# Two model stacks in one kernel: other orders in the recurrent block and in the second stack's attention, and splits moved or made narrower

## The reference

```python
gate, u = jnp.split(x @ w_in, 2, axis=-1)
u = causal_depthwise_conv(u, conv_w, conv_b)                 # 4 taps
r = sigmoid(blocks(u) @ w_rgate + b_rgate)                   # 4 blocks of 256 features
i = sigmoid(blocks(u) @ w_igate + b_igate)
log_a = -LRU_C * r * softplus(-lam)
b_in = sqrt(-expm1(2 * log_a)) * (i * u)
h_t = exp(log_a)_t * h_(t-1) + b_in_t                        # a scan over the tokens
y = (h * gelu(gate)) @ w_o
```

## Time and profile before

| | us |
|---|---|
| median of 3 runs | 2154.22 (2153.88 to 2158.78) |
| the profiled execution | 2156.41 |
| its span | 2155.1 |
| PE busy | 2062.3 (96%) |
| DVE busy | 1540.4 (71%) |
| ACT busy | 1177.7 (55%) |
| POOL busy | 68.5 (3%) |

### The profile page before, as it was taken

How to read it: one execution, slowest core, us unless ns; L and a number is a source line. 1 busy time by engine, 2 the same in 40 slices (tenths; PEclk the granted TensorE clock), 3 DMA queues, 4 the chain that set the end, 5 groups by cost and what they waited for, 6 DMA issues and landing times.

```text
span 2155.1 us, 33112 instructions
## 1 busy us (share of the span) xinstructions
PE 2062.3 (96%) x13325; PEld 1860.2 (86%) x13325; DVE 1540.4 (71%) x2678; ACT 1177.7 (55%) x2047; POOL 68.5 (3%) x121
## 2 busy tenths in 40 slices
PE   7999999898999989999998999999989999989998
PEld 7878899796899978889987789998978999878997
DVE  4685776888677776677777867778466777666776
ACT  4555555484465556456554545655455655565654
POOL 3000000010000010000000000001000000000000
PEclk9999999999999999999999999999999999999999
DMA  8424566455366654457654346665525765524763
GB/s 270 145 90 147 171 203 189 143 165 181 120 199 196 190 147 132 139 154 216 191 179 140 104 143 213 205 186 161 158 69 158 214 204 178 168 85 135 220 178 118
DMA packets 411849, 355.81 MB, mean 165 GB/s; under 512 B 16163, under 2 KB 353319, under 8 KB 411697
## 3 DMA queue, kind: packets, MB, share of 16 engines
q1 hardware_dynamic: 405104, 332.49, 50.5%
q0 software_dynamic: 6592, 21.21, 3.0%
HBM read 352.61 MB, written 1.05 MB: 164 GB/s over the span
## 4 chain that ended last, share of the span: by engine, by line
PE 80%; DVE 13%; ACT 4%; issue 1%; DMA 1%; POOL 0%; SPq 0%; DVEq 0%; ACTq 0%
PE psum L715 19%; PE psum L717 18%; PE psum L716 18%; PE psum L1228 15%; DVE w_lo L1825 3%; PE psum L1121 3%; PE psum L1107 1%; DVE qt L2260 1%; PE psum L1050 1%; ACT w_hi L1387 1%; DVE x_tok L2208 1%; PE psum L891 1%; DVE n_tok L2205 1%; PE psum L809 1%; DVE xt_lo L1860 1%
## 5 line engine op out<-in xcount | busy, mean ns | idle before, releaser
L1825 DVE TENSOR_TENSOR w_lo<-w_raw,w_hi 128x1024 fp32r<-128x1024 f32 x639 | 753.2, 1224 | 186.7 <-ACT w_hi L1387 186.1
L715 PE MATMUL psum<-xt_hi,w_hi 128*128 128x256 f32 x2424 | 690.6, 285 | 8.6 <-DVE w_lo L1825 8.1
L716 PE MATMUL psum<-xt_lo,w_hi 128*128 128x256 f32 x2424 | 687.8, 284 | 0.0
L717 PE MATMUL psum<-xt_hi,w_lo 128*128 128x256 f32 x2424 | 687.7, 284 | 0.0
L1387 ACT CAST w_hi<-w_raw 128x1024 fp32r<-128x1024 f32 x639 | 637.5, 1048 | 90.6 <-DMA w_raw<-in_f_w_up_dram 15.4
L715 PEld LDWEIGHTS psum<-xt_hi,w_hi 128*128 128x128 f32 x2424 | 466.7, 193 | 15.8 <-issue 7.9
L716 PEld LDWEIGHTS psum<-xt_lo,w_hi 128*128 128x128 f32 x2424 | 466.8, 193 | 4.8
L717 PEld LDWEIGHTS psum<-xt_hi,w_lo 128*128 128x128 f32 x2424 | 466.7, 193 | 0.0
L715 PE MATMUL psum<-w_hi,xt_hi 128*128 128x512 f32 (+4 forms) x860 | 326.3, 379 | 25.1 <-DVE xt_lo L1860 12.3
L717 PE MATMUL psum<-w_hi,xt_lo 128*128 128x512 f32 (+4 forms) x860 | 316.5, 368 | 0.0
L716 PE MATMUL psum<-w_lo,xt_hi 128*128 128x512 f32 (+4 forms) x860 | 316.1, 368 | 0.0
(11 more groups left out here) (223 smaller groups left out, 1871.2 us busy)
## 6 DMA issues: line engine op xcount, KB each, us to landing
w_raw<-in_f_w_up_dram SPq DMA_DIRECT2D x160, 512.0 KB, 5.3
w_raw<-in_f_w_down_dram SPq DMA_DIRECT2D x88, 512.0 KB, 3.6
w_raw<-in_w_up_dram SPq DMA_DIRECT2D x80, 512.0 KB, 5.3
w_raw<-in_w_down_dram SPq DMA_DIRECT2D x44, 512.0 KB, 3.6
w_raw<-in_x_w_q_dram SPq DMA_DIRECT2D x32, 512.0 KB, 4.2
w_raw<-in_x_w_o_dram SPq DMA_DIRECT2D x32, 512.0 KB, 4.8
w_raw<-in_a_w_qkv_dram SPq DMA_DIRECT2D x24, 512.0 KB, 4.7
w_raw<-in_w_in_fox_dram SPq DMA_DIRECT2D x20, 512.0 KB, 4.7
```

Of the source, the lines that this page charges most:

```text
L715: self.eng.matmul(out, stat[0], mov[0], start=first, stop=False)
L716: self.eng.matmul(out, stat[0], mov[1], start=False, stop=False)
L717: return self.eng.matmul(out, stat[1], mov[0], start=False, stop=last)
L1825: self.up(self.eng.tensor_tensor(self.m.lo[:, s, :], self.m.raw[:, u % RAW, :], self.m.hi[:, s, :].bitcast(F32), ALU.subtract), "w_lo", u)
```

## The change

- The weights' DMAs no longer wait for the memory rows, the identity has a semaphore of its own, and the first two feature tiles of `project_features` are made one after the other, both in one bank.
- A split works on the columns that the unit holds.
- In a feed-forward the last of the extra units is split after tile 21's work, not before it.
- The rates from lambda are made in ffn0 (tiles 8 to 10).
- The recurrent block starts with 512 features of u as token blocks (four units), with the late pieces of x turned between them; ACT copies the two blocks, TensorE transposes them back into feature tiles 0 to 3; then come feature tiles, sigmoid products and single gate tiles in a new order over all banks. The square of a moves from DVE to ACT, all splits to other places, and the first two pairs of output tiles are finished before the second half's scans.
- In the second stack the memory groups come first, all query and key tiles of layer 0 lie in the fills of steps 0 to 2 (two pairs each), the memory queries of layer 1 before the attention, and the output units are taken in the order 3, 0, 1, 2.

```diff
+CONV_BANKS = (4, 5, 1, 3, 0, 2, 6, 7)
+SIGMOID_BANKS = ((4, 5), (1, 3), (4, 5), (6, 7))
+RATES_STAGE, RATES_TILES = "ffn0", (8, 9, 10)
...
-def narrow_sums(e, c):
+def narrow_sums(e, c, units=(0, 1, 2, 3)):
+    if c == 0:
+        e.order = units
     if c in (5, 7):
-        e.sum_unit((c - 5) // 2)
+        e.sum_unit(units[(c - 5) // 2])
     elif c == 9:
-        e.sum_unit(2, (0,))
+        e.sum_unit(units[2], (0,))
     elif c == 10:
-        e.sum_unit(2, (1,))
+        e.sum_unit(units[2], (1,))
     elif c == 11:
-        e.sum_unit(3)
+        e.sum_unit(units[3])
...
 def forgetting(e):
     def fill(e, c):
         if c < 3:
-            e.forgetting_tiles(c + 3)
-        narrow_sums(e, c)
+            e.forgetting_tiles(2 * c)
+            e.forgetting_tiles(2 * c + 1)
+        narrow_sums(e, c, (3, 0, 1, 2))
     def settle(e, c):
         if c < 3:
-            e.keep_forgetting_tiles(c + 3)
+            e.keep_forgetting_tiles(2 * c)
+            e.keep_forgetting_tiles(2 * c + 1)
     e.forgetting_start()
-    attend(e, groups_of(FORGETTING, MEMORY), fill, settle)
+    attend(e, groups_of((MEMORY, D_MIX // P), (FORGETTING, 0)), fill, settle)
...
@@ def dilated(e): @@
         elif c == 2:
-            e.memory_queries()
             e.turn_late_keys()
-        narrow_sums(e, c)
+        narrow_sums(e, c, (3, 0, 1, 2))
...
-    attend(e, groups_of(DILATED, MEMORY), fill, settle)
+    attend(e, groups_of((MEMORY, D_MIX // P), (DILATED, 0)), fill, settle)
...
@@ Sync @@
+        self.counts[("w_columns", u)] = k * n
...
             self.landing(self.eng.dma_start(self.m.tok[:, b, :], self.t["mem"][b * P:(b + 1) * P, :]), "mem_in")
-        self.wait_ge("mem_in")
...
-        t, w = self.t, self.t["b_w_in"][0]
-        for blk in range(KT // 2):
-            self.features(w, D + 2 * blk * P, 2)
-            if blk > 0:
-                self.gate_weights(blk - 1)
-        self.features(w, 0, 2)
-        self.gate_weights(KT // 2 - 1)
-        self.features(w, 2 * P, KT - 2)
-        self.w_out = t["b_w_o"][0]
+        w = self.t["b_w_in"][0]
+        tile = lambda i, n=1: self.features(w, i * P, n)
+        self.tokens(w, D, BANK)
+        tile(KT + 4, 4)
+        self.gate_weights(0)
+        tile(0)
+        self.gate_weights(1)
+        tile(1)
+        self.gate_weights(2)
+        tile(2)
+        self.gate_weights(3)
+        tile(3, 5)
+        self.w_out = self.t["b_w_o"][0]
...
@@ Tensor @@
-        self.wait_ge("const_in")
+        self.wait_ge("ident_in")
...
     def project_features(self, what, tiles):
...
-        for j in range(2, tiles, 2):
+        for j in range(0, tiles, 2):
...
+        def turned_tile(i):
+            k = CONV_BANKS[i]
+            self.claim(k)
+            for b in range(TB):
+                self.wait_ge("kept", self.tag, "first", b)
+                ins = self.eng.transpose(m.psum[:, k, b * P:(b + 1) * P], m.n_tok[:, b, i * P:(i + 1) * P], m.ident[:])
+            self.up(ins, "made", self.tag, "u", i)
+            self.free[k] = ("conv", self.tag, i)
...
-        self.turn_now()
+        self.project_blocks("first", (6, 7), BANK)
+        conv_tile(4)
+        for i in range(4):
+            turned_tile(i)
+        for i in (5, 6, 7):
+            conv_tile(i)
         for blk in range(KT // 2):
-            conv_tiles(blk)
-            if blk > 0:
-                sigmoids(blk - 1)
-        gate_products(0)
-        sigmoids(KT // 2 - 1)
-        for j in range(1, KT // 2):
-            gate_products(j)
+            sigmoids(blk)
+            if blk < 3:
+                gate_products(blk)
+        for i in range(3, KT):
+            gate_products(i)
...
@@ Tensor.forgetting_tiles, dilated_start @@
-        self.feature_pair("qk", (1, 4, 5, 0, 1, 0)[g], g)
+        self.feature_pair("qk", 1 - g % 2, g)
...
         self.project_tokens("v1", (6, 7), D_MIX - BANK)
+        self.memory_queries()
...
@@ Scalar.split; Vector.split alike @@
-        self.up(self.eng.copy(self.m.hi[:, s, :], self.m.raw[:, u % RAW, :]), "w_hi", u)
+        n = self.counts.get(("w_columns", u), UNIT)
+        self.up(self.eng.copy(self.m.hi[:, s, 0:n], self.m.raw[:, u % RAW, 0:n]), "w_hi", u)
...
@@ Scalar.recurrent_block (new lines) @@
+            self.up(ins, "act", self.tag, "decays", q)
+            self.wait_ge("act", self.tag, "decays", q)
+            self.wait_ge("pool", self.tag, "gated_in", q)
+            self.up(self.eng.activation(u[:, h, :], r[:, h, :], ACT.Square), "exps", self.tag, q)
...
+        self.keep_first()
+        self.units()
+        for i in (4, 0, 1):
+            base(i)
+        self.units()
+        base(2)
+        base(3)
+        hidden(0)
+        self.units()
+        base(5)
+        self.units()
+        base(6)
+        base(7)
+        for blk in range(KT // 2):
+            sigmoids(blk, 0)
+            if blk < KT // 2 - 1:
+                hidden(blk + 1)
+            sigmoids(blk, 1)
+            if blk < KT // 2 - 1:
+                self.units(3)
+            if blk == 2:
+                tanhs(0)
+        tanhs(1)
+        self.units(3)
+        decays(0)
+        self.units()
+        decays(1)
+        self.units(2)
+        for q in range(2):
+            self.wait_ge("prod", self.tag, "one_minus", q)
+            self.up(self.eng.activation(th[:, halves[q], :], th[:, halves[q], :], ACT.Sqrt), "act", self.tag, "root", q)
+        gated(0)
+        gated(1)
+        high(0)
+        high(1)
+        self.units()
+        gated(2)
+        gated(3)
+        high(2)
+        high(3)
...
@@ Scalar.feed_forward; Vector.feed_forward alike @@
-            if q in down_tiles(FT):
+            if FT - HIDDEN <= q < FT - 1:
                 self.units()
             tile(q)
+            if q == RATES_TILES[1] and self.tag == RATES_STAGE:
+                self.rates()
...
+        self.units()
         if memory is not None:
...
@@ Vector.recurrent_block (its order) @@
+        self.units(KT // 2)
+        conv(0)
+        conv(1)
+        self.units()
+        hidden(0)
+        conv(2)
+        conv(3)
+        self.units(2)
+        conv(4)
+        self.units()
+        conv(5)
+        hidden(1)
+        self.units(3)
+        conv(6)
+        hidden(2)
+        self.units(3)
+        conv(7)
+        hidden(3)
+        self.units(3)
+        self.units(3)
+        decays(0)
+        self.units()
+        decays(1)
+        self.units(2)
+        states(0)
+        gated(0)
+        gated(1)
+        lowered(0)
+        lowered(1)
+        self.units()
+        states(1)
+        gated(2)
+        gated(3)
+        lowered(2)
+        lowered(3)
...
@@ Vector: decays, and the rates, which were at the block's head @@
             self.wait_ge("exps", self.tag, q)
-            self.wait_ge("pool", self.tag, "gated_in", q)
-            self.after(self.step(self.eng.tensor_tensor(u[:, h, :], r[:, h, :], r[:, h, :], ALU.mult)))
...
+    def rates_start(self):
+        ab = self.m.small[:, 0, 0:KT]
...
@@ Vector.forgetting_start @@
-        self.units(2 + 4)
+        self.units(2)
...
-        self.units(2)
@@ Pool.start @@
+        self.load(m.ident[:], t["c_ident"], "ident_in")
```

More of the change, by code:

```diff
@@ L237, in groups_of @@
 def groups_of(*attentions):
-    out, head, tile = [], 0, 0
-    for a in attentions:
+    out, head = [], 0
+    for a, tile0 in attentions:
         first = head
-        for _ in range(a.groups):
-            out.append(Group(len(out), a, first, head, tile))
+        for j in range(a.groups):
+            out.append(Group(len(out), j, a, first, head, tile0 + j * a.tiles))
             head += a.per
-            tile += a.tiles
     return out
@@ L282, in __init__ @@
         self.limit = None
+        self.order = range(HALF)
         self.tag = self.x = self.h = "start"
@@ L490, in program @@
             e.recurrent_block()
-            for j in range(KT // 2):
+            e.order = range(HALF)
+            for j in e.order:
                 e.sum_unit(j)
@@ L1406, in project_features @@
         m = self.m
-        self.units(2)
-        for a, k in enumerate((4, 5)):
-            self.wait_ge("made", self.tag, what, a)
-            self.keep(self.copies(dst, m.psum[:, k:k + 1, 0:SEQ], a, 1), what, a, scale=scale)
-        for j in range(2, tiles, 2):
+        for j in range(0, tiles, 2):
             self.units(2)
@@ new lines, in hidden, with sigmoids @@
+        def hidden(blk):
+            if blk > 0:
+                self.wait_ge("made", self.tag, "sig", blk - 1, 1)
+            self.wait_ge("conv", self.tag, 2 * blk + 1)
+            self.up(self.eng.copy(m.hid[0][:, 0:2, :], u[:, 2 * blk:2 * blk + 2, :]), "x_hi", self.tag, blk, 0)
+        def sigmoids(blk, q):
+            dst, bias = ((r, b_r), (ig, b_i))[q]
+            self.wait_ge("made", self.tag, "sig", blk, q)
+            for a in range(2):
+                jt = 2 * blk + a
```

(35 more changed lines are left out.)

201 lines of the change are left out of this document (79 added, 122 removed).

## The result

Three runs of the kernel before gave 2154.22 us; with the runs beside the changed kernel it is 2154.65 (2153.44 to 2158.78, 6 runs). The changed kernel took 2136.79 (2136.12 to 2139.07, 6 runs): a ratio of 0.991, 95% interval 0.990 to 0.992, so about 18 us faster. The forecast was 2133.8, range 2123 to 2145.

What follows compares the result with a forecast made beforehand. TensorE, busy 96% of the span, was taken as the bound, leaving its idle and lower-clock time to win. Gains of 2.4 + 3.3 + 6.0 + 0.5 + 4.5 + 3.7 = 20.4 us gave 2133.8, range 2123 to 2145.

Steps and rivals of the forecast that it cites:

- it lies 2.2 above the median: Last step of the total: profiled 2156.41 lies 2.2 above median 2154.22, so profiled 2136.0 becomes a median of 2133.8.
- The 0.4 for the identity's own semaphore: Start: TensorE no longer waits for rope_sin until 6.2, which brings the first product 0.4 us earlier.
- 3 us lost: Start, bad end of the range: two megabytes of weights slow the two memory transfers, 3 us lost.
- The 0.1 that I had taken off for the later split: Feed-forward ends: DVE's first normalisation step comes later behind the moved split, leaving a cost of 0.1 us.
- about 1 us: Recurrent middle: ACT and DVE keep up with TensorE but for about 1 us, conv tiles 6 and 7 coming late.
- a hole in the middle: Sign against the forecast: a hole inside the recurrent block's middle would prove the sum wrong.
- The dearer case: Recurrent middle: GpSimd's product also catches the split of hid; 2.1 us more, sum 18.3 instead of 20.4.
- last two end at 501.1: Recurrent tail: the last two output units end at 501.1, against 507.1 before, a gain of 6.0 us.
- Rival: the clock: Smaller, closer holes keep the 0.50 stretches; 1.6 and 2.6, and some 2 us at the recurrent front, lost: 2140; chance 0.10.
- The slower rival: Paired q and k copies on ACT delay the next splits in layer 0 and four recurrent blocks: 2166; chance 0.05.
- the turned sums: Second-stack layer 0: a wait of 0.6 us, since their cover of one feature tile goes.
- The 0.5 for late keys: Second-stack layer 1: a wait of 0.5 us, late keys being rotated with no query tile over them.

Runs made afterwards that it cites:

- kept_busy: Changed kernel plus 72 extra unused products in TensorE's 9.7 us hole at the end of the recurrent block; ratio to the kernel before 0.9900.
- memory_last: Changed kernel with the second stack's memory groups last again, tile, query and output-unit order of before included; 2146.65 us, ratio to the kernel before 0.9949.
- sinks_and_order: Changed kernel with second-stack features split ahead of weight units, and the sliding layers' sinks' copy behind the start's last splits; 2126.95 us, ratio to the kernel before 0.9863.
- moved kernel: Changed kernel with sliding-layer zeroing and sinks' copy later, one recurrent unit split after the second scans, second-stack features split before weights; 2135.00 us.
- start_dma_back: Changed kernel with first-layer weights queued only after the memory rows and the identity on the shared constants' semaphore again; ratio to the kernel before 0.9902.
- start_turns_back: Changed kernel with the first layer's first two units multiplied alternately again, weights still queued at once; ratio to the kernel before 0.9910.
- recurrent_back: Changed kernel with the recurrent block of before, decay rates at its head again; ratio to the kernel before 0.9919.

## Why the prediction was right, and where it was not

**Total.** The sum was 20.4 us; the two profiled executions differ by 20.3. That it is so close is luck: the terms miss by +0.7 (start), +0.5 (feed-forwards), -0.8 (recurrent block), -0.8 (layer 3) and 0.1 or 0.2 in each of the rest, which cancel, and single runs of either kernel differ by 3 to 5 us. What missed by 3.0 us is the last step, "it lies 2.2 above the median": I took the distance of the profiled run of before to its median and assumed it for the changed kernel too, whose profiled run is its fastest, 0.7 below the median. 2.2 + 0.7 and the 0.1 of the sum are the 3.0.

**Start.** First product forecast at 12.5 to 12.9, measured 12.88. The 0.4 for the identity's own semaphore did not come: TensorE started at 6.28 against 6.2, released by the identity itself, which landed no earlier than rope_sin had, since the weights now came beside it. What the prediction missed is that rope_sin itself landed at 9.63, so that by the estimate above the semaphore saved about 3 us, a risk that the prediction had not counted. The other end, "3 us lost" by slower memory rows, came to 0.4 (6.01 for 5.62). The stage gave 3.1: 2.0 by the first product, and the rest fits the lower clock, which I had left out and which held 3.4 us instead of 6.9.

**Feed-forward ends.** 1.2 to 1.3 each for a forecast of 1.1. The 0.1 that I had taken off for the later split was not there.

**Recurrent block.** Front: holes of 0.55, 0.29 and 0.70, none over 1.5, as forecast. With the 5.4 went the lower clock behind it (416.7 to 426.9 before), which the sum didn't price by itself. Middle: 1.5 us of holes for "about 1 us", 0.28 at 449.78 and 1.26 at 464.63, behind the last sigmoids. The larger one came, by the rows, not from the splits of the conv tiles but from the tanh ahead of three units. The prediction had called a hole in the middle a proof that the sum is wrong; one came and the sum held, because about 1 us was in it already. So that sign was set too strictly. GpSimd's product overlapped the splits as I had counted:

```profile
446.67 2.42 POOL L2524 TENSOR_TENSOR e<-e,kt 128x1024 f32<-128x1024 f32 x1 [27.66 <-ACT e L1532]
```
```profile
445.88 0.69 DVE L1889 TENSOR_TENSOR hid_lo<-kt,hid_hi 128x512 fp32r<-128x512 f32 x1 [0.31 <-ACT hid_hi L1525]
447.13 4.25 DVE L1874 TENSOR_TENSOR w_lo<-w_raw,w_hi 128x512 fp32r<-128x512 f32 x3 [0.56 <-ACT w_hi L1402]
```

Two of the three splits have 512 columns (0.69) and one 1024 (1.23), 2.6 us together; they took 4.25. The rest, 1.65, is about what GpSimd still had to do at 447.13 (1.96): one by one, the first split took 2.50 us for 0.69, until 449.63, and GpSimd ended at 449.09. The rule of the Trainium skill, *SBUF — State Buffer*, Who interferes with whom (the two exclude each other for a whole instruction), agrees with that. The prediction read its own row of before a little wrong: of the two splits in 449.25 and 4.57 the first took the usual 1.22, and the second, from 450.38 to 453.82, was the one held beside GpSimd. The dearer case that the prediction drew from the rule did not come about, because the split of hid ended before GpSimd began, and the wait left for TensorE was 0.28. Tail: restart 74.1 after the first transpose for 74.7, second scans 81.9 for 82.4, and TensorE ran through from 483.25 to 506.39. So the step "last two end at 501.1" held to within about half a microsecond. What failed is what I did not price behind it: the norm. TensorE waited 1.28 us for x_tok. By the rows (no run tried it) DVE did four splits in a row (491.70 to 496.3), the next weights were issued as these ended, DVE stood 1.17 for a high half that waited 1.91 for them, so the first norm step came at 498.64, and the third at 504.09 stood behind two more splits (from 501.65), the first of whose high halves had waited 3.10 for its weights. That is why 6.0 became 5.2. Seen from the block's first transpose, TensorE's restart came 7.4 earlier (74.2 for 81.6), and 2.2 of that were lost behind it: the second scans and the norm set the pace there.

**Rival: the clock.** I had the low clock in the tail as part of the working and priced none of it as loss; kept_busy shows that to be right. In the second stack I priced it at 1.6 and 2.6 beside waits of 2.9 and 1.1. The sums came out (4.6 and 4.0 in memory_last for 4.5 and 3.7), the parts less well: 5.3 of waits for 4.0 and some 3.3 of clock for 4.2. The slower rival (copies of q and k tiles late in each step) did not come: no w_lo is among the waits of layer 0's first steps.

**Second stack.** No wait for the exponentials (ACT's e) is left. The mask waits came as forecast (0.84 three times, 0.74 three times, for 0.93 and 0.8), the turned sums 0.56 for 0.6, the memory queries 0.68 for 0.7, the last transposes 0.92 for 0.75 in layer 0 and 0.33 for 0.7 in layer 1. The 0.5 for late keys did not appear. In layer 1, then, waits gave 2.2 where 1.1 was forecast.

**Latent layer.** 0.6 for 0.5, but this isn't shown to be the narrow splits: with the same code the stage takes 94.3 to 95.0 in six traces, and 94.9 before.

**Layer 3.** The -0.8 there is the sinks' DMA: 8 KB, issued at 1127.20, for which DVE stood until 1133.05, in front of four splits. The stage varies from 95.1 to 96.2 in kernels with the same code, so it can't be called a cost of the change. DVE stood 2.17 for the same DMA before; that the wait was avoidable in the changed kernel, sinks_and_order shows.

## What to carry to other kernels

Ask of every hole what would be late right after it: filling the clock's dip in the recurrent tail gained nothing, since the next thing came no sooner. On an engine with one queue, a short instruction that waits for a DMA, or a bulk one that nobody needs yet, belongs behind what the busiest engine waits for; moving it has to be checked against the next consumer too (the keys' rotation, the norm), as two of three moves lost what they gained or more. A transfer that is queued earlier makes others land later: look at who waits for those. When a sum is built on one profiled run, compare it with another profiled run; the distance to a median isn't carried over.

## What the hardware showed that I had not expected

In the moved kernel TensorE went from the level of 1.00 to 0.50 in the midst of 48 products of 12 columns (0.11 us each), 3.5 us after the first of them, with a hole of only 0.58 ahead and no other between; the products left then took 0.21 each. In sinks_and_order the level fell 4.2 us after the first, at 1487.9, behind a hole of 0.57, and stayed low until 1494.7.

Low stretches of 3.4 us come and go between traces of the same code. In layer 0 one is there at 64.5 (start_dma_back) and 65.0 (start_turns_back), behind a hole of 1.0, and the stage takes 89.8 us; without it, 88.7. In the latent layer four traces have one near 791 to 794, behind holes of 1.8 to 2.8, and take 95.7 to 97.1; the six without it have holes of 1.6 to 2.2 there and take 94.3 to 95.0. Such a stretch is a good part of the spread between runs, and is not to be read as an effect of the edit under test.

One load of 8 KB, the sinks' in layer 3, was waited for until 4.8 us behind its issue in one trace (recurrent_back) and 5.85 in another (the changed kernel), which made TensorE's hole behind it 1.51 or 2.58.
